# A two-layer hybrid backbone kernel: its first modulation in four half blocks of 512 outputs, with products two parts at a time

## The reference

```python
silu_c, silu_cc = jax.nn.silu(c), jax.nn.silu(c_ctx)
ada_lat = silu_c @ ada_w[l] + ada_b[l]          # 1024 -> 6 * 1024
ada_ctx = silu_cc @ ada_w[l] + ada_b[l]
...
h = rms_norm(x, lp["ln1"]) * (1.0 + sc1) + sh1   # latent tokens
hc = rms_norm(xc, lp["ln1"]) * (1.0 + csc1) + csh1
z = h @ w_in                                     # the first products
```

## Time and profile before

| | |
|---|---|
| median of 3 runs | 2125.05 us (2125.02 to 2125.42) |
| profiled execution: its time | 2125.46 us |
| profiled execution: span of the trace | 2123.7 us |
| PE busy | 2085.4 us, 98% of the span |
| DVE busy | 1279.5 us, 60% |
| ACT busy | 522.4 us, 25% |
| POOL busy | 900.9 us, 42% |

### The profile page before, as it was taken

One profiled execution on the slowest core, in us unless ns is written; L12 is line 12 of the kernel. 1 busy time (PEld: TensorE's weight loads), 2 busy tenths in 40 slices (PEclk: granted clock), 3 DMA queues, 4 the chain that ended last, 5 costly groups with the idle time before them and its releaser, 6 DMA issues.

```text
span 2123.7 us, 30482 instructions
## 1 busy us (share of the span) xinstructions
PE 2085.4 (98%) x12276; PEld 1887.2 (89%) x12276; DVE 1279.5 (60%) x2126; ACT 522.4 (25%) x862; POOL 900.9 (42%) x492
## 2 busy tenths in 40 slices
PE   6999999999999999999999999999999999999998
PEld 5999999877799999999999999888777788888887
DVE  6997992455663679677787743793266756122223
ACT  4115122465401230211201221412365213010011
POOL 2541443200144264444444443454511456666663
PEclk9999999999999999999999999999999999999999
DMA  7363345233352154543545417345400632322222
GB/s 289 107 142 106 118 158 172 94 116 119 131 182 95 50 193 160 208 158 132 196 148 176 162 60 222 107 179 168 137 26 25 210 105 90 109 92 97 99 99 70
DMA packets 110431, 281.95 MB, mean 133 GB/s; under 512 B 23210, under 2 KB 45098, under 8 KB 108510
## 3 DMA queue, kind: packets, MB, share of 16 engines
q1 hardware_dynamic: 74544, 206.60, 28.8%
q10 hardware_dynamic: 35758, 73.50, 10.6%
HBM read 241.72 MB, written 37.88 MB: 132 GB/s over the span
## 4 chain that ended last, share of the span: by engine, by line
PE 91%; DVE 6%; ACT 1%; issue 1%; DMA 0%; POOL 0%; ACTq 0%; DVEq 0%; SPq 0%; POOLq 0%
PE ps L511 65%; PE ps L624 5%; PE ps L1222 3%; PE ps L1096 2%; PE ps L1236 2%; PE ps L1272 2%; PE ps L646 2%; PE ps L1122 1%; PE ps L1134 1%; PE ps L650 1%; PE ps L702 1%; PE ps L1169 1%; PE ps L951 1%; PE ps L1085 1%; DVE t_in L2487 1%
## 5 line engine op out<-in xcount | busy, mean ns | idle before, releaser
L1457 POOL TENSOR_SCALAR whi<-raw 128x1024 fp32r<-128x1024 f32 x244 | 270.9, 1110 | 1173.4 <-PE ps L511 679.0
L1460 POOL TENSOR_TENSOR wlo<-raw,whi 128x1024 fp32r<-128x1024 f32 x244 | 630.6, 2585 | 20.4
L511 PE MATMUL ps<-hh,whi 128*128 128x384 f32 (+1 forms) x1512 | 450.0, 353 | 1.3 <-DVE zs L2121 1.3
L511 PE MATMUL ps<-hl,whi 128*128 128x384 f32 (+1 forms) x1512 | 447.6, 351 | 0.0
L511 PE MATMUL ps<-hh,wlo 128*128 128x384 f32 (+1 forms) x1512 | 447.5, 351 | 0.0
L511 PEld LDWEIGHTS ps<-hh,whi 128*128 128x128 f32 x1512 | 275.4, 188 | 21.3 <-DVE zs L2121 1.7
L511 PEld LDWEIGHTS ps<-hl,whi 128*128 128x128 f32 x1512 | 276.5, 188 | 18.6 <-issue 0.2
L511 PEld LDWEIGHTS ps<-hh,wlo 128*128 128x128 f32 x1512 | 276.3, 188 | 18.4
L511 PE MATMUL ps<-midh,whi 128*128 128x384 f32 (+1 forms) x672 | 201.9, 354 | 2.1 <-DVE x L2425 2.1
L511 PE MATMUL ps<-midl,whi 128*128 128x384 f32 (+1 forms) x672 | 200.9, 353 | 0.0
L511 PE MATMUL ps<-midh,wlo 128*128 128x384 f32 (+1 forms) x672 | 200.8, 352 | 0.0
(11 more groups left out here) (302 smaller groups left out, 3408.3 us busy)
## 6 DMA issues: line engine op xcount, KB each, us to landing
raw<-in_w_main SPq DMA_DIRECT2D x244, 512.0 KB, 3.3
dot_w<-in_ada_dot SPq DMA_DIRECT2D x80, 512.0 KB, 4.3
ada_mixer<-in_ada_w SPq DMA_DIRECT2D x24, 512.0 KB, 4.0
g_d<-gt ACTq DMA_DIRECT2D x24, 384.0 KB, 2.4
gl<-g_d ACTq DMA_DIRECT2D x8, 1152.0 KB, 5.6
ada_first<-in_ada_w SPq DMA_DIRECT2D x16, 512.0 KB, 14.6
cout_d<-cz SPq DMA_DIRECT2D x12, 512.0 KB, 4.8
cout<-cout_d ACTq DMA_DIRECT2D x6, 1024.0 KB, 8.6
```

Source lines behind the costliest of these rows:

```text
L511: ins = pe.matmul(bank(p, h, a, b), ww[:, w % W_SLOTS, kw * P:(kw + 1) * P], xx[:, kx, a:b], start=(first and i == 0 and j == 0), stop=(la ...
L1457: pool.tensor_scalar(whi[:, u, :], raw[:, u % 2, :], 1.0, 0.0, ALU.mult, ALU.add).then_inc(w_split.sem, 1)
L1460: pool.tensor_tensor(wlo[:, u, :], raw[:, u % 2, :], whi[:, u, :].bitcast(F32), ALU.subtract).then_inc(w_split.sem, 1)
```

## The change

Blocks 0 and 1 become four half blocks of 512 outputs: half block i holds shift and scale of parts 2i and 2i+1. It takes 4 steps instead of 8, and a step covers two slices of the inner dimension: of its four matmuls of 256 columns two belong to each slice, and the partial sums of the two slices lie on different partition groups until the turn adds them, by a matrix `pick_two` with ones at both. A step is still four matmuls and 512 KB, and there are still 16. Every half block has its own row copy, turn, bias and gain. The first half block is turned before the root is spread. DVE makes the products for `nt` and `hl` two parts at a time, and PE's order has steps 4 to 15 and the turns of half blocks 1 to 3 between the parts of weight tiles 0 and 1; tile 2 starts with parts 0 to 5 alone. The load of weight tile 1 is issued after modulation tile 3 instead of after 7. In layer 1 the first gain is made in four instructions instead of two. The diff, cut to its core (left out: where the tiles lie in SBUF, the order of `ada_w` in memory, and the index arithmetic of the gain):

```diff
@@ -670,27 +671,66 @@
             key = (0, 1)
             pe.wait_ge(diag_ready.sem, diag_ready.at(key))
             pe.matmul(ps[:, 3, 0:512], ones[:, :], diag[:, 0:512], start=True, stop=True)
-            pe_ada(pe, 6)
-            pe_ada(pe, 7)
             pe.matmul(ps[:, 3, 512:TOK], ones[:, :], diag[:, 512:TOK], start=True, stop=True).then_inc(
                 rstd_spread.sem, rstd_spread.mark(key))
-            pe_turn(pe, 0)
...
+        def first_home(i):
+
+            o = ps[:, 2, 512 * (i % 2):512 * (i % 2) + 512]
+            return o[:, 0:256], rows_first[:, i % 2], o[:, 256:264].rearrange("p (q j c) -> p q j c", q=2, c=2)
+
+        def pe_first(pe, s):
+
+            i, u = divmod(s, 4)
+            sums = first_home(i)[0]
+            if u == 0 and i >= 2:
+                pe.wait_ge(ada_row.sem, ada_row.at(("first", i - 2)))
+                pe.wait_ge(ada_ready.sem, ada_ready.at(("gain", 0, 0, 2 * (i - 2))))
+            pe.wait_ge(ada_full[s].sem, ada_full[s].at(s))
+            for k in range(2):
+                for j in range(2):
+                    r = 32 * (2 * k + j)
+                    ins = pe.matmul(sums[r:r + 32], svec[:, 2 * u + k, :], ada_first[s][:, 512 * k + 256 * j:512 * k + 256 * j + 256],
+                                    start=(u == 0), stop=(u == 3))
+            ins.then_inc(ada_used.sem, ada_used.mark(("first", s)))
...
+        def pe_first_turn(pe, i):
+
+            _, rows, o = first_home(i)
+            if i == 0:
+                pe.wait_ge(ones_ready.sem, ones_ready.at("pick"))
+            pe.wait_ge(ada_row.sem, ada_row.at(("first", i)))
+            for q in range(2):
+                ins = pe.matmul(o[:, q], rows[:, q * P:(q + 1) * P], pick_two[:, :, :], start=True, stop=True, skip_group_check=True)
+            ins.then_inc(ada_turned.sem, ada_turned.mark(("first", i)))
+
+        def act_first_rows(act, i):
+
+            sums, rows, _ = first_home(i)
+            act.wait_ge(ada_used.sem, ada_used.at(("first", 4 * i + 3)))
+            if i >= 2:
+                act.wait_ge(ada_turned.sem, ada_turned.at(("first", i - 2)))
+            act.copy(rows, sums).then_inc(ada_row.sem, ada_row.mark(("first", i)))
+
+        def dve_first(dve, i):
+
+            o = first_home(i)[2]
+            dve.wait_ge(ada_turned.sem, ada_turned.at(("first", i)))
+            dve.tensor_tensor(ada[:, 0, 4 * i:4 * i + 4, :].rearrange("p (j q) c -> p q j c", q=2), o,
+                              ada_b[:, 0, 4 * i:4 * i + 4].rearrange("p (j q) -> p q j", q=2).unsqueeze(3).to_broadcast(
+                                  [P, 2, 2, 2]), ALU.add).then_inc(ada_ready.sem, ada_ready.mark(("first", i)))
+            dve.wait_ge(ada_ready.sem, ada_ready.at(("first", i)))
...
+            for k in range(0, KD, 2):
+                dve_gain(dve, 1, 0, k, k + 2, 2)
             for k in (0, KD // 2):
-                dve_gain(dve, 1, 0, k, k + KD // 2, 2)
                 dve_gain(dve, 1, 1, k, k + KD // 2, 1)
...
                 for i in range(2):
                     low_step(pe, i, i, 0, TOK)
-                for k, steps in ((0, range(8, 11)), (1, range(11, 13)), (2, range(13, 16))):
-                    if k:
-                        first_tiles(range(2), k)
-                    for s in steps:
-                        pe_ada(pe, s)
-                pe.wait_ge(hi_ready.sem, hi_ready.at((0, 1, 3)))
-                for i in range(2):
-                    high_step(pe, i, i, 3, TOK)
-                pe_turn(pe, 1)
-                pe.wait_ge(lo_ready.sem, lo_ready.at((0, 1, 3)))
-                for i in range(2):
-                    low_step(pe, i, i, 3, TOK)
+                for s in (4, 5):
+                    pe_first(pe, s)
+                first_tiles(range(2), 1)
+                for i in (1, 2):
+                    for s in range(4 * i + 2, 4 * i + 4):
+                        pe_first(pe, s)
+                    pe_first_turn(pe, i)
+                    first_tiles(range(2), 2 * i)
+                    for s in range(4 * i + 4, 4 * i + 6):
+                        pe_first(pe, s)
+                    first_tiles(range(2), 2 * i + 1)
+                for s in range(14, 16):
+                    pe_first(pe, s)
+                pe_first_turn(pe, 3)
                 wait_w(pe, 2)
-                pe.wait_ge(ada_ready.sem, ada_ready.at(("gain", 0, 0, 4)))
-                for k in range(4):
+                pe.wait_ge(ada_ready.sem, ada_ready.at(("gain", 0, 0, 6)))
+                for k in range(6):
                     first_tiles((2,), k)
-                for k in range(4, KD):
+                for k in range(6, KD):
                     first_tiles(range(3), k)
                 tile(3, 3)
...
             for s in range(2):
-                pe_ada(pe, s)
+                pe_first(pe, s)
             pe_first_sums(pe)
-            for s in range(2, 6):
-                pe_ada(pe, s)
+            for s in range(2, 4):
+                pe_first(pe, s)
+            pe_first_turn(pe, 0)
             pe_first_spread(pe)
...
-            for step in range(2):
+            for step in range(2 * KD):
                 load_ada(step)
-            load_w(0)
-            for step in range(2, KD):
-                load_ada(step)
-            load_w(1)
-            for step in range(KD, KD + 4):
-                load_ada(step)
-            load_w(2)
-            for step in range(KD + 4, 2 * KD):
-                load_ada(step)
+                if step in (1, 3, 11):
...
             if l == 0:
-                for k in range(KD // 2):
-                    act_hi(act, 0, 1, TOK, k)
-                act.dma_start(s5[0].b_in[:], A["ssm_b"][0]).then_inc(prep_loaded.sem, prep_loaded.mark(0, 16))
-                act_rows(act, 1)
-                for k in range(KD // 2, KD):
-                    act_hi(act, 0, 1, TOK, k)
+                for i in range(4):
+                    if i:
+                        act_first_rows(act, i)
+                    if i == 2:
+                        act.dma_start(s5[0].b_in[:], A["ssm_b"][0]).then_inc(prep_loaded.sem, prep_loaded.mark(0, 16))
+                    for k in range(2 * i, 2 * i + 2):
+                        act_hi(act, 0, 1, TOK, k)
...
             act_first_root(act)
+            act_first_rows(act, 0)
             step_sizes(act, 0)
             magnitudes(act, 0)
             sines(act, 0)
-            act_rows(act, 0)
...
             if l == 0:
-                dve_norm(dve, 0, 1, TOK, 0, KD // 2)
-                doubled(dve, 0, 1)
-                doubled(dve, 0, 2)
-                dve_ada(dve, 1)
-                first_gain(dve, 1)
-                dve_norm(dve, 0, 1, TOK, KD // 2, KD)
+                for i in range(4):
+                    if i:
+                        dve_first(dve, i)
+                        first_gain(dve, i)
+                    dve_norm(dve, 0, 1, TOK, 2 * i, 2 * i + 2)
+                    if i in (0, 1):
+                        doubled(dve, 0, i + 1)
...
-            for i in range(2):
+            for i in range(4):
                 first_gain_constant(dve, i)
+            dve.tensor_tensor(pick_two[:, :, :], pick[:, 0:2], pick[:, 2:4], ALU.add).then_inc(
+                ones_ready.sem, ones_ready.mark("pick"))
             for k in range(1, KD):
                 add_squares(dve, (0, 1), k, TOK)
             first_invert(dve)
+            dve_first(dve, 0)
+            first_gain(dve, 0)
             coefficients(dve, 0)
             transition(dve, 0)
-            dve_ada(dve, 0)
```

More of the change, by code:

```diff
@@ L118, in ada_tile @@
 def ada_tile(row, k):
-    return (k // 4) * 8 + 4 * row + k % 4 if row < 2 else row * KD + k
+    return (k // 2) * 4 + 2 * row + k % 2 if row < 2 else row * KD + k
 FULL = 4
@@ L213, in build @@
         root_h = const("root_h", [P, 2, 6])
+        pick_two = const("pick_two", [P, 2, 2])
         raw = at("raw", RING, [P, RAW_SLOTS, KD * P])
@@ L329, in build @@
         binT = at("binT", EXTRA + 11648, [P, SG, 2, P])
-        first_at = ([HREG + 4096 * j for j in (0, 1, 2, 6, 7, 8)] + [REST + 89088, REST + 93184]
-                    + [HREG + 4096 * j for j in (3, 4, 5, 9, 10, 11)] + [REST + 105472, REST + 109568])
+        first_at = ([HREG + 4096 * j for j in (0, 1, 6, 7, 2, 8)] + [REST + 89088, REST + 93184]
+                    + [HREG + 4096 * j for j in (3, 4, 9, 10, 5, 11)] + [REST + 105472, REST + 109568])
         ada_first = [at(f"ada_first{j}", o, [P, D]) for j, o in enumerate(first_at)]
@@ L672, in pe_first_spread @@
             pe.matmul(ps[:, 3, 0:512], ones[:, :], diag[:, 0:512], start=True, stop=True)
-            pe_ada(pe, 6)
-            pe_ada(pe, 7)
             pe.matmul(ps[:, 3, 512:TOK], ones[:, :], diag[:, 512:TOK], start=True, stop=True).then_inc(
                 rstd_spread.sem, rstd_spread.mark(key))
-            pe_turn(pe, 0)
         pick = ident[:, :].rearrange("p (j s) -> p j s", s=32)[:, :, 0:2]
         def ada_home(i):
-            if i < ADA_FIRST:
```

(44 more changed lines are left out.)

## The result

The change took 2143.88 us (median of 6 runs, 2143.40 to 2144.63) against 2124.48 us before (6 runs, 2123.65 to 2125.42): ratio 1.009, 95% interval 1.008 to 1.010. It is slower by 19.4 us, where 9.7 were forecast with a range up to 2140.5. The profiled executions differ by 18.0 us of span, of which 17.75 are there when tile 4 starts.

A forecast was written before the change was run, and what follows sets the result against it. PE was taken to bound the kernel; -0.95 + 2.0 + 8.0 + 1.83 - 1.34 = +9.5 us, up to +9.9 with seams, taken as +9.7 on 2125.05: 2134.8 us, range 2131 to 2140.5.

The forecast's parts named there:

- the walk of the prediction: PE's times added up from the first product at 27.85 us to tile 4 at 79.1, against 69.19 before.
- The pauses at the turns: PE ahead of parts 2 and 4: 4.18 us each, together 8.0 more than before; ahead of tile 2, 1.83.
- DVE in time for tile 4: Ahead of tile 4: PE's 1.34 us wait for DVE's `zs` goes, if DVE is in time.
- The head start: First product: starts at 27.85 us instead of 28.81, 0.95 us earlier, with bounds of 0.4 to 1.5.
- no obstacle: Weight tile 1 ahead of the first product: its load stands 5.1 us earlier and was claimed not to hold anything up.
- I take full rate, from that row: PE behind its pauses: stays at full rate, since 2.4 us of waiting before the first product had not brought half rate back.
- The price per place: Half rate behind the first product or any of three turns: at most 2.6 us each, likely 1.5 to 2.
- Two signs that the prediction had named for being wrong: `nt` starting under 25 or past 27 us; matmuls after a pause near 0.35 us apart instead of 0.17.
- The rival that the low rate bites: Half rate behind one or more of four places: one gives 2136.5 us, three 2140 to 2141; chance 0.35.

The follow-up runs named there:

- The first experiment: The change with only PE's order rewritten, so the low product and the next four steps stand behind each of turns 1 and 2: 2130.94 us.
- The fill run: The change plus matmuls whose results nobody reads, put behind the spread and the turns so PE is not idle in the pauses: 2138.03 us.
- coefficients late: The change with `coefficients`, `transition` and their small functions moved behind the first pair on DVE and ACT: 2140.07 us.
- both edits: The change with PE's rewritten order and with `coefficients` and `transition` moved behind the first pair, together: 2128.58 us.

## Why the prediction was wrong

Right were the direction, the place and the mechanism of the largest term. Against the walk of the prediction, which put tile 4 at 79.1 (+9.9), it started at 86.94, which is 17.75 us later than before. The terms:

- **The pauses at the turns**, forecast 4.18 us each: step 7 to part 2 took 35.90 + 1.04 = 36.94 to 41.14, 4.20; at half block 2 it was 4.1; ahead of tile 2 1.8 as forecast. Right. The first experiment shows them, with the low rate behind them, as the main cause: with the turns covered 12.9 of the 19.4 us were gone.
- **DVE in time for tile 4, -1.34**: right, there is no wait for `zs`.
- **The head start, -0.95**: it came out as +0.19 (29.00 against 28.81). The chain was right (turn, coefficients, transition, `nt`), but I timed the block of `coefficients` and `transition` from a trace in which POOL stood idle beside it. Now POOL's split of tile 1, which the change's earlier load brings forward, holds its first instruction up by 0.9 us. The rest is that `coefficients` started at 22.86 and not at 22.6, behind a step 3 that ended at 20.69 (20.54 forecast) and a turn at the low rate of 1.0 us. I named the earlier load and counted it only as "no obstacle". That this load made the hold-up is shown by the run that moved it, which also shows that undoing it only moves the hold-up to `pw`.
- **The step that failed: "I take full rate, from that row".** Part 0 lost 3.61 - 2.62 = 1.0 us; part 2 and its two steps took 41.14 to 46.04, 4.90 in place of 3.29, 1.6; part 4 and its steps 53.48 to 59.40, 5.92 in place of 3.29, 2.6; tile 2's six parts 8.05 in place of 6.24, 1.8: together 7.0 us. With the 1.15 us of the head start that is the difference to the walk, 7.8, within 0.4. The fill run gives 5.9 us of it back by itself. The row that I went by, full rate after 2.4 us of waiting, was one pause; the three large pauses of the change were 0.7 to 1.6 us longer. That it was their length is not shown: the low rate also followed ahead of tile 2, where PE was idle for only 0.49 and 0.71 us around a turn. The price per place, "at most 2.6, likely 1.5 to 2", was about right (1.0, 1.6, 2.6 and 1.8); the chance was not. Two signs that the prediction had named for being wrong came: `nt` past 27 (27.35) and matmuls after a pause 0.32 us apart. The range left out three or four such places, and it was four.

The rival that the low rate bites is thus what happened. The rule of the Trainium skill that stood beside it ("TensorE: Matmul & The Clock Gate", Part 1, "What's actually happening": the throttled state is the default and that of an idle array, and activity releases it) was the better guide here; one pause in the trace before was too little to set against it. The hold-up by POOL has its rule in the Trainium skill too ("SBUF — State Buffer", "Who interferes with whom"): a VectorE instruction with two SBUF inputs contends with a GpSimd instruction that reads SBUF. These traces agree, with 0.2 us turned to 1.09 in the change and to 1.91 in the run that moved the load, each time until the split had ended.

## What to carry to other kernels

Cutting a gating computation into smaller blocks costs time where the waiting engine has no other work written behind each block's hand-over; with such work in place it only came out even here. Count the chain from the hand-over to the first use (here 3.1 us from the end of the turn, through DVE and ACT), and put at least that much of the engine's own work between. A pause on PE was charged twice here, once as itself and once in the rate of the work behind it. So a forecast of a new pause of 3 to 4 us in a kernel like this one should have that second charge (here 1.0 to 2.6 us a place) in its sum, not among the rivals. And a block that is moved is to be timed with what will run beside it.

## What the runs showed of the hardware

The idle time ahead of eight high products of one part, and what they took, in the profiled executions:

| run, place | idle ahead, us | eight products, us |
|---|---|---|
| first product, coefficients late | 1.77 | 1.65 |
| part 2, both edits | 1.98 | 2.19 |
| first product, before | 2.38 | 1.66 |
| part 2, the change | 0.49, a turn, 3.14 | 2.20 |
| part 2, tile 1 loaded as before | 0.49, a turn, 3.14 | 2.93 |
| part 4, the change | 0.49, a turn, 3.06 | 2.93 |
| first product, the change | 4.02 | 2.90 |
| first product, turns covered | 4.01 | 2.90 |
| parts 2 and 4, turns covered | 0.48, 0.39 | 1.66 |

There is no clean bound: 1.98 us was followed by the low rate and 2.38 us was not. The same pauses did not always cost the same either: ahead of part 2 they were followed by 2.20 us in one run and by 2.93 us in another, and ahead of tile 2 (0.49 us, a turn, 0.70 us) its six parts took 8.05 us in the change and 6.51 us with tile 1 loaded as before:

```profile
67.72:74.23 6.51, 6.50 (x37) 6.51 (x38) 6.13 (x16) 2.18 (x4) 0.00 (x0) 1.00 0.21 28
```

What decides besides the length is open. The granted clock of the profile is not a complete witness either. The first product with the turns covered took 2.90 us, yet its stretch reads 1.00:

```profile
29.17:33.16 3.99, 3.99 (x16) 3.74 (x20) 3.69 (x12) 1.38 (x3) 0.00 (x0) 1.00 1.02 408
```

So does the stretch up to 22 us in every run, in which PE works at half rate (two steps take 1.9 us, against 1.0 later). The distance between equal matmuls tells the rate; the clock column can miss it.
